# One 2 MB transfer for both up tiles of a group, and the down tiles' transfers issued from ScalarE's own queue

## The chip, the cores and the metric

One core of one Trainium2 chip. The time is device microseconds for one launch. Engines are named as in the profile: PE is TensorE's matmul side, PEld its weight loads, DVE is VectorE, ACT is ScalarE, POOL is GpSimd and SP is SyncE. "SPq" and "ACTq" are the parts of SyncE and ScalarE that issue DMA transfers.

## The reference

A first block (two layers of three kinds of attention) is followed by a second one of two layers with four token mixers each. The first of these has a dense feed-forward, the second a mixture of 8 experts in which each of 256 tokens goes to its best two. All data is 32-bit float. The change touches the mixture alone:

```python
logits = h @ router_w                       # 256 tokens, 8 experts
top_vals, top_idx = lax.top_k(logits, TOP_K)   # TOP_K = 2, softmax over the two
# every expert: (silu(h @ w1) * (h @ w3)) @ w2, D_MODEL = 1024, EXPERT_FF = 2816
```

The weights of the 8 experts are 8 x 3 x 1024 x 2816 x 4 bytes, 277 MB, and all of them are read once.

## The kernel before, in words

The mixture is the last stage. An expert's hidden width of 2816 is cut into 11 groups of 256 columns, so there are `UPS` = 88 groups. A group has three weight tiles of 128 partitions x 2048 floats (1 MB each, 8 KB of a row per partition): two *up* tiles (`w1` and `w3` for the first and the second half of the 1024 input features) and one *down* tile (`w2`). There are 264 tiles in all, numbered in the order in which PE uses them: `up_tile(g, 0)`, `up_tile(g, 1)`, then `down_tile(g - 2)`. So PE runs, in step g: the ups of group g, one transpose (`turn`) of the activations of group g-1, and the down of group g-2. ACT takes the tanh of a group when its ups are done, DVE multiplies the gates, ACT copies the transposed activations.

The experts are taken by rank of how many tokens they have (`TURN`). Of the eight turns, the third and the sixth are *heavy*: their expert has room for 128 tokens and not for 64, and its weights are cut in two parts, a rounded one made by ACT (L1020) and the rest made by DVE (L1200), for three matmuls in place of one. The other six turns are *light*. In time: two light turns (22 groups), one heavy (11), two light, one heavy, two light.

The tiles live in a ring of `RAW` = 12 places of 1 MB; four more places (`HI`) are used once, for the first 16 tiles. SyncE issues every transfer itself, in the order of the tiles, on its own queue (L981 to L994): tile n waits until PE has finished tile n-12 (n-16 for the first tiles behind the first 16). Each engine keeps its order of work; semaphore `m_done` counts the tiles that PE has finished. A transfer goes out as soon as its place is free:

```python
if n < FIRST:
    sp.wait_ge(family("m_done"), p * (TILES + FIRST) + n + 1)
else:
    sp.wait_ge(*tile_done(p, n - (FIRST if n < FIRST + RAW else RAW)))
src = ...
sp.dma_start(raw[slot_of(n)], src).then_inc(raw_loaded(p, n)[0], 16)
```

The first 12 places come free together in the last projection of the stage in front, at one increment of `m_done` by 12; the four of `HI` at another.

Of the kernel before, what the change touches and what calls it, by code (L numbers as in the profile page):

```python
# [17 lines left out]
P = 128  # L18
D = 1024
# [22 lines left out]
TURN = [0, 3, 1, 4, 5, 2, 6, 7]  # L42
PASSES = max(-(-min(SEQ, 2 * SEQ // max(r, 1)) // n) for r, n in enumerate(ROOMS))
W2B = 384
RAW = 12
HI = 4
FIRST = RAW + HI
HALF = NF // 2
# [84 lines left out]
def build(nc, a, consts, out, events):  # L133

    ccols, _, c_shared, c_first = constants()
    with ExitStack() as ctx:
# [179 lines left out]
        raw, raw_r = map(list, zip(*[carve_both(2048) for _ in range(6)]))  # L316
        top[0] = mark
        for i in range(5):
            raw.append(mem_ring[:, 2048 * i:2048 * (i + 1)])
            raw_r.append(carve_both(2048)[1])  # L320
# [3 lines left out]
        raw.append(mem_ring[:, top[0] - at_ring:top[0] - at_ring + 2048])  # L324
        raw_r.append(carve_both(2048)[1])
        assert top[0] <= after_z + c_all - c_first
        top[0] = 0
        assert len(raw_r) == RAW
        raw_hi, hi_r = map(list, zip(*[carve_both(2048) for _ in range(3)]))
        raw += raw_hi  # L330
# [3 lines left out]
        raw.append(sq.rearrange("p a b -> p (a b)")[:, 0:2048])  # L334
        assert len(hi_r) == HI
        he_f, he_h = high_places(KT, P)
        he = [carve(KT, GROUP) for _ in range(2)]
# [419 lines left out]

            return sum(heavy(k) for k in range(i))

        def slot_of(n):  # L760

            return n if n < FIRST else (n - FIRST) % RAW

        def raw_loaded(p, n):

            k = slot_of(n)
            if k >= RAW:
                last = max(range(k - RAW, len(chunks), NSLOT))
                s, before = at(f"w_loaded{k - RAW}", last)
                return s, p * 16 + before + 16  # L770
            loads = len(range(k, TILES - FIRST, RAW)) + 1
            return family(f"m_raw{k}"), p * 16 * loads + 16 * (1 if n < FIRST else (n - FIRST) // RAW + 2)

        def split_done(p, n):

# [10 lines left out]
        def moe_pe(pe, logit, open_group):  # L786
# [60 lines left out]
            def up(p, g):  # L847

                i, c = divmod(g, HALF)
                if g >= 2:  # L850
                    pe.wait_ge(family("m_hidden"), p * UPS + g - 1)
                for half in range(2):
                    n = up_tile(g, half)
                    if c == 0:
                        pe.wait_ge(family("m_he"), p * 2 * EXPERTS + 2 * i + (half + 1 if heavy(i) else 2))
                    if heavy(i):
                        pe.wait_ge(*split_done(p, n))
                        high, low = hi_r[SPLIT.index(n) % HI], raw_r[slot_of(n)]
                        for k in range(4):
                            kk = 4 * half + k  # L860
                            for j, (h_, w_) in enumerate(((he_h, high), (he_h, low), (he_l, high))):
                                ins = pe.matmul(ACC[g % 2][:, :], h_[:, kk, :], w_[:, 512 * k:512 * k + 512],  # L862
                                                start=(kk == 0 and j == 0), stop=(kk == KT - 1 and j == 2))
                    else:
                        pe.wait_ge(*raw_loaded(p, n))
                        for k in range(4):
                            kk = 4 * half + k
                            for f in range(2):
                                ins = pe.matmul(ACC[g % 2][64 * f:64 * f + 64, 0:2 * P], he[i % 2][:, kk, :],  # L869
                                                raw[slot_of(n)][:, 512 * k + 256 * f:512 * k + 256 * (f + 1)],  # L870
                                                start=(kk == 0), stop=(kk == KT - 1), skip_group_check=True)
                    ins.then_inc(family("m_done"), 1)

# [7 lines left out]
            def down(p, d):  # L881

                i, c = divmod(d, HALF)
                n = down_tile(d)
                pe.wait_ge(family("m_act"), p * UPS + d + 1)
                if c == 0 and i:
                    pe.wait_ge(family("m_y"), p * EXPERTS + i)
                if heavy(i):
                    pe.wait_ge(*split_done(p, n))
                    pe.wait_ge(family("m_act_low"), p * HEAVY * HALF + heavy_before(i) * HALF + c + 1)  # L890
                    high, low = hi_r[SPLIT.index(n) % HI], raw_r[slot_of(n)]
                    for f in range(2):
                        for half in range(2):
                            at_ = f * D + 512 * half
                            for j, (a_, w_) in enumerate(((act_h, high), (act_h, low), (act_l, high))):
                                ins = pe.matmul(SB[half][:, :], a_[:, d % 2, f * P:(f + 1) * P], w_[:, at_:at_ + 512],  # L896
                                                start=(c == 0 and f == 0 and j == 0),
                                                stop=(c == HALF - 1 and f == 1 and j == 2))
                else:
                    pe.wait_ge(*raw_loaded(p, n))  # L900
                    for f in range(2):
                        for half in range(2):
                            ins = pe.matmul(SB[0][64 * half:64 * half + 64, :], act_t[:, d % 2, GROUP * f:GROUP * (f + 1)],  # L903
                                            raw[slot_of(n)][:, f * D + 512 * half:f * D + 512 * half + 512],
                                            start=(c == 0 and f == 0), stop=(c == HALF - 1 and f == 1),
                                            skip_group_check=True)
                ins.then_inc(family("m_done"), 1)
# [69 lines left out]
        def moe_sync(sp):  # L977

            def body(p, learn):
                expert = {0: 0}  # L980
                for n in range(TILES):  # L981
                    g, j = TILE_ORDER[n]
                    i, c = divmod(g, HALF)
                    if i not in expert:
                        r = TURN[i]
                        if i == 1:
                            sp.wait_ge(*at("passes_known"))
                        expert[i] = sp.value_load(by_rank[0:1, r:r + 1], min_val=0, max_val=EXPERTS - 1)
                    if n < FIRST:
                        sp.wait_ge(family("m_done"), p * (TILES + FIRST) + n + 1)  # L990
# [4 lines left out]
                    if n == 2 * TILES // EXPERTS:  # L995
                        learn()
                        sp.dma_start(gain_row, a["final_norm_g_2"].rearrange("(r d) -> r d", r=1).broadcast_to((P, D)))\
                            .then_inc(family("m_gain_row"), 16)
            turns(sp, body)

        def moe_act(act):
# [13 lines left out]
            def high(p, n):  # L1015

                at_ = SPLIT.index(n)
                act.wait_ge(*raw_loaded(p, n))
                act.wait_ge(*tile_done(p, SPLIT[at_ - HI] if at_ >= HI else FIRST - 1))
                cp(hi_r[at_ % HI], raw[slot_of(n)]).then_inc(family("m_high"), 1)  # L1020

            def expert_in(p, i):

# [14 lines left out]
                ins.then_inc(family("m_y"), 1)  # L1038

            def body(p, learn):  # L1040
                for s in range(UPS + 2):
                    i, c = divmod(s, HALF)
                    if s == 2 * HALF:
# [6 lines left out]
                    if 1 <= s <= UPS:  # L1050
# [2 lines left out]
                        A(hid[g % 2][:, 0:n * P].rearrange("p (a b) -> p a b", a=n),  # L1053
                          ACC[g % 2][:, 0:2 * n * P].rearrange("p (a b) -> p a b", a=n)[:, :, 0:P], ACT.Tanh, scale=0.5)\
                            .then_inc(family("m_tanh"), 1)
                    if c == 2 and i:
                        y_out(p, i - 1)
                    if c == 9 and i + 1 < EXPERTS:
# [22 lines left out]
        def moe_dve(dve, st):  # L1081
# [114 lines left out]
            def low(p, n):  # L1196

                at_ = SPLIT.index(n)
                dve.wait_ge(family("m_high"), p * len(SPLIT) + at_ + 1)
                TTn(raw_r[slot_of(n)], raw[slot_of(n)], hi_f[at_ % HI], ALU.subtract).then_inc(family("m_split"), 1)  # L1200

            def expert_in(p, i):

# [1896 lines left out]
```

## Time and profile before

| | |
|---|---|
| median of 3 runs | 2174.63 us (2174.55 to 2176.81) |
| the profiled execution | 2175.69 us, span 2173.9 us |
| the mixture's weight stream | first issue at 1486.49, last tile's down matmuls begin at 2159.55 |
| PE busy in the span | 2070.3 us (95%) |
| DMA rate in the mixture | about 420 GB/s, against 225 GB/s over the span |

Times in the profile are microseconds from the start of the span. "DMA share" is the mean busy share of the core's 16 DMA engines and can be a little over 1, since packets overlap. For a DMA issue the profile gives the time from issue to landing, for which the transfers queued ahead of it on the same queue count too.

### The profile page before, as it was taken

Reading aid. Unit: us, or ns where it says so; the run is one execution under the profiler, and the core shown is the slowest. Engines: PE = TensorE matmul, PEld = TensorE weight load, DVE = VectorE, ACT = ScalarE, POOL = GpSimd, SP = SyncE. Lnnn points to the kernel's source line nnn. Section 1 sums busy time; section 2 is a strip of 40 time slices with the busy share of each in tenths; the row PEclk is TensorE's granted clock in tenths of the full one; section 3 lists DMA queues with packets and bytes.
Section 4 is the critical chain, followed back from the end, with each engine's and each line's share of the span. In section 5 each row is a group of like instructions: output and inputs, shape, how many; then the busy total and the mean of one; then the engine's idle time right before and its main releaser. Section 6 shows DMA issues by size and latency. Waiting matters only on the chain. (4 is left out here: it accounts for less than half of the span.)

```text
span 2173.9 us, 38831 instructions
## 1 busy us (share of the span) xinstructions
PE 2070.3 (95%) x15492; PEld 1737.7 (80%) x15492; DVE 1270.5 (58%) x2412; ACT 946.6 (44%) x1724; POOL 124.9 (6%) x115
## 2 busy tenths in 40 slices
PE   8999999999999999998999899998999999999997
PEld 7988888998978988888999888888556765568553
DVE  5465667565667776778665775777114931178211
ACT  5545544545554453446443544444014630065111
POOL 0100000010000024021000005012000000000000
PEclk9999999999999999999999999999999999999999
DMA  6443334444337444346554444339999999999997
GB/s 198 151 136 101 98 98 140 145 144 136 113 123 163 142 152 131 106 137 219 172 191 137 138 147 145 107 118 346 392 421 420 421 413 420 420 421 407 409 420 310
DMA packets 257818, 489.49 MB, mean 225 GB/s; under 512 B 35256, under 2 KB 208216, under 8 KB 223720
## 3 DMA queue, kind: packets, MB, share of 16 engines
q1 hardware_dynamic: 252112, 484.39, 61.6%
q8 instruction: 124, 2.03, 0.4%
q0 software_dynamic: 656, 1.80, 0.2%
q10 hardware_dynamic: 4872, 0.81, 0.2%
q14 instruction: 54, 0.44, 0.1%
HBM read 485.91 MB, written 1.05 MB: 224 GB/s over the span
## 5 line engine op out<-in xcount | busy, mean ns | idle before, releaser
L1356 PE MATMUL bank<-memr 128*128 128x256 f32 (+3 forms) x7056 | 896.6, 286 | 28.4 <-DVE memr L2417 9.7
L1356 PEld LDWEIGHTS bank<-memr 128*128 128x128 f32 (+2 forms) x7056 | 855.5, 185 | 58.8 <-issue 16.3
L2417 DVE TENSOR_TENSOR memr<-mem_low,memr 128x1024 fp32r<-128x1024 f32 (+3 forms) x328 | 400.0, 1238 | 63.8 <-ACT memr L1864 63.1
L1864 ACT CAST memr<-mem_low 128x1024 fp32r<-128x1024 f32 (+3 forms) x328 | 333.3, 1032 | 112.7 <-PE bank L1356 109.8
L1252 DVE SCALAR_TENSOR_TENSOR mem_high<-mem_high,bank 128x128 f32<-128x128 f32 (+1 forms) x88 | 28.0, 318 | 273.4 <-ACT mem_high L1053 273.4
L1053 ACT ACTIVATE mem_high<-bank 128x128 f32<-128x128 f32 (+1 forms) x88 | 26.7, 304 | 348.1 <-PE bank L869 322.8
L869 PE MATMUL bank<-mem_tail,mem_low 128*64 128x256 f32 x1088 | 127.5, 387 | 2.9 <-DMA mem_tail<-in_moe 2.3
L869 PEld LDWEIGHTS bank<-mem_tail,mem_low 128*64 128x64 f32 x1088 | 77.9, 139 | 54.2 <-issue 17.3
L660 PE MATMUL bank<-memr 128*128 128x256 f32 x960 | 115.6, 281 | 3.1 <-DVE memr L2436 3.1
L869 PE MATMUL bank<-mem_ring,mem_low 128*64 128x256 f32 x992 | 113.7, 381 | 3.7 <-DMA mem_ring<-in_moe 3.7
L660 PEld LDWEIGHTS bank<-memr 128*128 128x128 f32 x960 | 114.3, 189 | 3.5 <-issue 3.5
L869 PEld LDWEIGHTS bank<-mem_ring,mem_low 128*64 128x64 f32 x992 | 70.2, 137 | 49.3 <-issue 15.3
L862 PE MATMUL bank<-memr 128*128 128x512 f32 x272 | 91.2, 404 | 6.5 <-DVE memr_tail L1200 6.5
L2179 ACT ACTIVATE mem_high<-bank 128x256 f32<-128x256 f32 x64 | 24.4, 382 | 127.9 <-PE bank L1356 127.9
L2047 ACT ACTIVATE mem_high<-mem_high 128x144 f32<-128x144 f32 (+2 forms) x120 | 51.0, 425 | 58.9 <-DVE mem_high L2601 58.9
L1356 PE MATMUL bank<-memr_ring,memr 128*128 128x256 f32 (+2 forms) x540 | 71.0, 288 | 4.3 <-ACT mem_high L2026 3.6
L1200 DVE TENSOR_TENSOR memr_tail<-mem_tail,memr 128x2048 fp32r<-128x2048 f32 x26 | 59.3, 2287 | 26.9 <-ACT memr L1020 26.5
L1356 PEld LDWEIGHTS bank<-memr_ring,memr 128*128 128x128 f32 (+1 forms) x540 | 66.3, 181 | 8.9 <-issue 2.8
L862 PEld LDWEIGHTS bank<-memr 128*128 128x128 f32 x272 | 52.3, 192 | 22.3 <-DVE memr_tail L1200 7.6
L903 PE MATMUL bank<-mem_ring,mem_low 128*64 128x512 f32 x264 | 63.9, 605 | 1.5 <-DMA mem_ring<-in_moe 1.1
L629 PE MATMUL bank<-memr_ring 128*128 128x256 f32 x416 | 64.4, 282 | 0.0
L903 PE MATMUL bank<-mem_tail,mem_low 128*64 128x512 f32 x248 | 60.0, 604 | 1.1 <-ACT mem_low L1063 1.1
(367 smaller groups left out, 2815.6 us busy)
## 6 DMA issues: line engine op xcount, KB each, us to landing
mem_tail<-in_moe SPq DMA_DIRECT2D x132, 1024.0 KB, 15.4
mem_ring<-in_moe SPq DMA_DIRECT2D x128, 1024.0 KB, 16.2
mem_low<-in_w_in SPq DMA_DIRECT2D x112, 1024.0 KB, 5.2
mem_tail<-in_ffn_w SPq DMA_DIRECT2D x18, 1024.0 KB, 8.6
mem_low<-in_w_out SPq DMA_DIRECT2D x16, 1024.0 KB, 5.3
mem_low<-in_w_branch SPq DMA_DIRECT2D x12, 1024.0 KB, 5.0
mem_high<-in_ffn_w SPq DMA_DIRECT2D x12, 1024.0 KB, 8.1
mem_low<-in_w_branch SPq DMA_DIRECT2D x16, 512.0 KB, 3.5
```

Of the source, the lines that this page charges most:

```text
L629: ins = pe.matmul(YB[j // 2][:, (j % 2) * T:(j % 2 + 1) * T], w_[:, j * P:(j + 1) * P], a_, start=(F == 0 and j % 2 == 0 and i == 0), stop ...
L660: ins = pe.matmul(UB[F % 2][m][:, 0:T], w_[:, k, :], h_[:, k, 0:T], start=(k == 0 and i == 0), stop=(k == KT - 1 and i == (2 if F else 1)))
L862: ins = pe.matmul(ACC[g % 2][:, :], h_[:, kk, :], w_[:, 512 * k:512 * k + 512], start=(kk == 0 and j == 0), stop=(kk == KT - 1 and j == 2))
L869: ins = pe.matmul(ACC[g % 2][64 * f:64 * f + 64, 0:2 * P], he[i % 2][:, kk, :], raw[slot_of(n)][:, 512 * k + 256 * f:512 * k + 256 * (f + 1)],
L903: ins = pe.matmul(SB[0][64 * half:64 * half + 64, :], act_t[:, d % 2, GROUP * f:GROUP * (f + 1)], raw[slot_of(n)][:, f * D + 512 * half:f ...
L1053: A(hid[g % 2][:, 0:n * P].rearrange("p (a b) -> p a b", a=n), ACC[g % 2][:, 0:2 * n * P].rearrange("p (a b) -> p a b", a=n)[:, :, 0:P], A ...
L1200: TTn(raw_r[slot_of(n)], raw[slot_of(n)], hi_f[at_ % HI], ALU.subtract).then_inc(family("m_split"), 1)
L1252: S3(out=hid[2 + g % 2][:, 0:n * P].rearrange("p (a b) -> p a b", a=n), in0=hid[g % 2][:, 0:n * P].rearrange("p (a b) -> p a b", a=n), sca ...
L1356: ins = pe.matmul(out(bank), lhsT, rhs, start=((k, i) == order[0] and not half), stop=((k, i) == order[-1]), skip_group_check=half is not ...
L1864: cp(high, raw).then_inc(*sig("w_high", i))
L2047: st(A(sm[g % 2][0:nt, c:c + n], sm[g % 2][0:nt, c:c + n], ACT.Exp, scale=sc, bias=s_[0:nt, 3 + t:4 + t], accum_out=s_[0:nt, 6 + t:7 + t]) ...
L2417: st(V.tensor_tensor(low, raw, high, ALU.subtract), sig("w_split", i))
```

## The change

The two up tiles of a group lie side by side in memory on both sides, so that one transfer brings both: 2 MB, with rows of 16 KB per partition. The ring becomes four places for pairs and four for down tiles (`PAIRS` = 4, the same 12 MB); the four extra places hold pairs 4 and 5, once. SyncE issues the pairs, and the first four down tiles. Pair g waits until PE has finished *both* up tiles of the pair that held its place before, that of group g-4 (g-6 for groups 6 to 9), and both up tiles wait for the whole pair. Down tile g of group 4 and on is issued by ScalarE on its own queue in step g, behind the tanh of group g-1. It waits for nothing further, since by then PE has finished down tile g-4. In a heavy step ScalarE has two casts (L1020) of that step's up tiles ahead of the tanh.

```diff
-RAW = 12
+PAIRS = 4
+RAW = 3 * PAIRS
+LOAD_ORDER = [n for n in range(TILES) if TILE_ORDER[n][1] == 0 or TILE_ORDER[n][1] == 2 and TILE_ORDER[n][0] < PAIRS]
+LOAD_ORDER.sort(key=lambda n: (FIRST if PAIRS <= TILE_ORDER[n][0] < PAIRS + HI // 2 and TILE_ORDER[n][1] == 0 else n, n))
...
+        def pair_of(g):
+            return g if g < PAIRS + HI // 2 else (g - PAIRS - HI // 2) % PAIRS
...
         def raw_loaded(p, n):
-            k = slot_of(n)
...
+            g, j = TILE_ORDER[n]
+            if j == 2:
+                return family(f"m_down{g % PAIRS}"), 16 * (p * UPS // PAIRS + g // PAIRS + 1)
+            k = pair_of(g)
...
+            of_place = [q for q in range(UPS) if pair_of(q) == k]
+            return family(f"m_up{k}"), 16 * (p * len(of_place) + of_place.index(g) + 1)
+
+        def expert_of(eng, i):
+            r = TURN[i]
+            if i == 1:
+                eng.wait_ge(*at("passes_known"))
+            return eng.value_load(by_rank[0:1, r:r + 1], min_val=0, max_val=EXPERTS - 1)
...
-                for n in range(TILES):
+                for n in LOAD_ORDER:
...
+                    k = pair_of(g)
+                    if j < 2 and g >= PAIRS + HI // 2:
+                        sp.wait_ge(*tile_done(p, up_tile(max(q for q in range(g) if pair_of(q) == k), 1)))
                     else:
-                        sp.wait_ge(*tile_done(p, n - (FIRST if n < FIRST + RAW else RAW)))
-                    src = a["moe"][bass.DynSlice(expert[i], 1), c, j].rearrange("o p f -> (o p) f") if i else a["moe"][0, c, j]
-                    sp.dma_start(raw[slot_of(n)], src).then_inc(raw_loaded(p, n)[0], 16)
+                        sp.wait_ge(family("m_done"), p * (TILES + FIRST) + (FIRST if j < 2 and k >= PAIRS else RAW))
+                    if j == 2:
+                        sp.dma_start(single[g], weights(expert, i, c, 2)).then_inc(raw_loaded(p, n)[0], 16)
+                    elif k > PAIRS:
+                        for half in range(2):
+                            sp.dma_start(last_raw[half], weights(expert, i, c, 0)[:, 2048 * half:2048 * (half + 1)])\
+                                .then_inc(raw_loaded(p, n)[0], 16)
+                    else:
+                        sp.dma_start(wide_hi[:, 0:4096] if k == PAIRS else pair[k], weights(expert, i, c, 0))\
+                            .then_inc(raw_loaded(p, n)[0], 16)
...
                 for s in range(UPS + 2):
...
                             .then_inc(family("m_tanh"), 1)
+                    if PAIRS <= s < UPS:
+                        if i not in expert:
+                            expert[i] = expert_of(act, i)
+                        act.dma_start(single[s % PAIRS], weights(expert, i, c, 2)).then_inc(raw_loaded(p, down_tile(s))[0], 16)
```

## Rows read from the trace of the kernel before

**Rows 1.** Page, busy time of the engines over the span; DMA rate in 40 slices.

```profile
PE 2070.3 (95%) x15492; PEld 1737.7 (80%) x15492; DVE 1270.5 (58%) x2412; ACT 946.6 (44%) x1724; POOL 124.9 (6%) x115
GB/s 198 151 136 101 98 98 140 145 144 136 113 123 163 142 152 131 106 137 219 172 191 137 138 147 145 107 118 346 392 421 420 421 413 420 420 421 407 409 420 310
```

**Rows 2.** Windows: first heavy turn, second heavy turn, the stream's last stretch.

```profile
1669.00:1768.00 99.00, 98.58 (x476) 77.70 (x476) 82.14 (x75) 63.02 (x57) 0.00 (x0) 1.00 1.01 419
1910.00:2019.00 109.00, 108.39 (x508) 84.33 (x509) 87.43 (x79) 67.69 (x62) 0.00 (x0) 0.97 1.01 411
2132.00:2160.00 28.00, 23.08 (x145) 10.49 (x146) 2.50 (x8) 3.74 (x11) 0.00 (x0) 1.00 0.91 377
```

**Rows 3.** Chain that ended last: start, duration, work (or transfer waited for).

```profile
1639.41 25.35 DMA mem_tail<-in_moe
...
1878.80 27.16 DMA mem_tail<-in_moe
```

**Rows 4.** DMA view of 1800 to 1860, the queue's packets, MB and share.

```profile
q1 hardware_dynamic: 3455, 25.17, 100.9%
```

**Rows 5.** DMA view of 649.4 to 653.8, and window 650.5 to 652.5.

```profile
q0 software_dynamic: 127, 1.56, 83.5%
...
650.50:652.50 2.00, 1.59 (x14) 1.39 (x12) 1.90 (x3) 1.06 (x1) 0.00 (x0) 1.00 1.01 433
```

**Rows 6.** Timeline of SP, single issues: start, duration of issuing.

```profile
1486.49 0.34 SPq L994 DMA_DIRECT2D mem_tail<-in_moe  x1
...
1530.73 0.33 SPq L994 DMA_DIRECT2D mem_tail<-in_moe  x1
...
1561.05 0.33 SPq L994 DMA_DIRECT2D mem_tail<-in_moe  x1
...
1566.76 0.34 SPq L994 DMA_DIRECT2D mem_tail<-in_moe  x1
...
1736.88 0.33 SPq L994 DMA_DIRECT2D mem_tail<-in_moe  x1
...
1749.04 0.33 SPq L994 DMA_DIRECT2D mem_tail<-in_moe  x1
...
1757.59 0.33 SPq L994 DMA_DIRECT2D mem_ring<-in_moe  x1
...
1979.52 0.33 SPq L994 DMA_DIRECT2D mem_tail<-in_moe  x1
...
1988.13 0.33 SPq L994 DMA_DIRECT2D mem_tail<-in_moe  x1
...
2000.24 0.33 SPq L994 DMA_DIRECT2D mem_ring<-in_moe  x1
...
2008.87 0.33 SPq L994 DMA_DIRECT2D mem_ring<-in_moe  x1
...
2023.39 0.33 SPq L994 DMA_DIRECT2D mem_tail<-in_moe  x1
...
2132.68 1.93 SPq L994 DMA_DIRECT2D mem_ring<-in_moe  x1
```

**Rows 7.** Issue to landing, of those at 1486.49, 1566.76, 1736.88, 1979.52 and 2023.39.

```profile
mem_tail<-in_moe SPq DMA_DIRECT2D x1, 1024.0 KB, 4.8
...
mem_tail<-in_moe SPq DMA_DIRECT2D x1, 1024.0 KB, 9.5
...
mem_tail<-in_moe SPq DMA_DIRECT2D x1, 1024.0 KB, 13.5
...
mem_tail<-in_moe SPq DMA_DIRECT2D x1, 1024.0 KB, 11.3
...
mem_tail<-in_moe SPq DMA_DIRECT2D x1, 1024.0 KB, 7.9
```

**Rows 8.** Timeline of PE at the stream's end: last up tile, last two downs.

```profile
2152.05 1.95 PE L869 MATMUL bank<-mem_tail,mem_low 128*64 128x256 f32 x16 [0.45 <-DMA mem_tail<-in_moe]
...
2159.55 1.94 PE L903 MATMUL bank<-mem_ring,mem_low 128*64 128x512 f32 x8 [0.51 <-DMA mem_ring<-in_moe]
```

More of the change, by code:

```diff
@@ L315, in build @@
         top[0] = upper
-        raw, raw_r = map(list, zip(*[carve_both(2048) for _ in range(6)]))
+        pair, pair_r = map(list, zip(*[carve_both(4096) for _ in range(3)]))
         top[0] = mark
-        for i in range(5):
-            raw.append(mem_ring[:, 2048 * i:2048 * (i + 1)])
-            raw_r.append(carve_both(2048)[1])
+        pair.append(mem_ring[:, 0:4096])
+        pair_r.append(carve_both(4096)[1])
+        single, single_r = [], []
+        for i in range(2, 5):
+            single.append(mem_ring[:, 2048 * i:2048 * (i + 1)])
+            single_r.append(carve_both(2048)[1])
         htok = [carve(D)]
@@ L323, in build @@
         top[0] = -(-(after_z + ccols["decay"][0] - c_first) // 8) * 8
-        raw.append(mem_ring[:, top[0] - at_ring:top[0] - at_ring + 2048])
-        raw_r.append(carve_both(2048)[1])
+        single.append(mem_ring[:, top[0] - at_ring:top[0] - at_ring + 2048])
+        single_r.append(carve_both(2048)[1])
         assert top[0] <= after_z + c_all - c_first
         top[0] = 0
-        assert len(raw_r) == RAW
-        raw_hi, hi_r = map(list, zip(*[carve_both(2048) for _ in range(3)]))
-        raw += raw_hi
+        assert len(pair_r) == len(single_r) == PAIRS
+        wide_hi, wide_hi_r = carve_both(6144)
+        hi_r = [wide_hi_r[:, 2048 * i:2048 * (i + 1)] for i in range(3)]
         hi_f = [v.bitcast(F32) for v in hi_r]
@@ L333, in build @@
         hi_r.append(memr_squares[:, 0:2048])
[L334 removed]
+        last_raw = wide_hi[:, 4096:6144], sq.rearrange("p a b -> p (a b)")[:, 0:2048]
         assert len(hi_r) == HI
@@ L758, in heavy_before, with raw_tile, raw_tile_r, weights @@
             return sum(heavy(k) for k in range(i))
-        def slot_of(n):
-            return n if n < FIRST else (n - FIRST) % RAW
-        def raw_loaded(p, n):
-            k = slot_of(n)
[L767 to L772, printed above, removed]
+        def pair_of(g):
+            return g if g < PAIRS + HI // 2 else (g - PAIRS - HI // 2) % PAIRS
+        def raw_tile(n, singles=single, pairs=pair, rest=(wide_hi[:, 0:4096], last_raw)):
+            g, j = TILE_ORDER[n]
+            if j == 2:
+                return singles[g % PAIRS]
+            k = pair_of(g)
+            if k > PAIRS:
+                return rest[1][j]
+            return (rest[0] if k == PAIRS else pairs[k])[:, 2048 * j:2048 * (j + 1)]
+        def raw_tile_r(n):
+            return raw_tile(n, single_r, pair_r)
+        def raw_loaded(p, n):
+            g, j = TILE_ORDER[n]
+            if j == 2:
+                return family(f"m_down{g % PAIRS}"), 16 * (p * UPS // PAIRS + g // PAIRS + 1)
+            k = pair_of(g)
+            if k >= PAIRS:
+                last = max(range(k - PAIRS, len(chunks), NSLOT))
+                s, before = at(f"w_loaded{k - PAIRS}", last)
+                return s, before + 16 * (k - PAIRS + 1) * (p + 1)
+            of_place = [q for q in range(UPS) if pair_of(q) == k]
+            return family(f"m_up{k}"), 16 * (p * len(of_place) + of_place.index(g) + 1)
+        def weights(expert, i, c, j):
+            lo, f = (0, 4096) if j < 2 else (P * 4096, 2048)
+            if i == 0:
+                return a["moe"][0, c, lo:lo + P * f].rearrange("(p f) -> p f", f=f)
+            return a["moe"][bass.DynSlice(expert[i], 1), c, lo:lo + P * f].rearrange("o (p f) -> (o p) f", f=f)
+        def expert_of(eng, i):
[3 more added lines that the diff above has]
+            return eng.value_load(by_rank[0:1, r:r + 1], min_val=0, max_val=EXPERTS - 1)
         def split_done(p, n):
@@ L1040, in body @@
             def body(p, learn):
+                expert = {0: 0}
                 for s in range(UPS + 2):
@@ L3080 @@
     w1, w3, w2 = (arrays.pop(f"moe_w{i}_2")[0] for i in (1, 3, 2))
[L3081 removed]
+    moe = np.empty((EXPERTS, HALF, 3 * P * 2048), np.float32)
+    ups, downs = moe[..., 0:P * 4096].reshape(EXPERTS, HALF, P, 2, 4, 2, 2, P), moe[..., P * 4096:]
     for m, w in enumerate((w1, w3)):
[L3083 to L3085 removed]
+        ups[..., m, :] = w.reshape(EXPERTS, 2, 4, P, HALF, 2, P).transpose(0, 4, 3, 1, 2, 5, 6)
+    downs[:] = w2.reshape(EXPERTS, HALF, 2, P, D).transpose(0, 1, 3, 2, 4).reshape(EXPERTS, HALF, P * 2 * D)
     arrays["moe"] = moe
```

28 lines of the change are left out of this document (11 added, 17 removed).

## The prediction

> **What bounds the kernel now.** First the page. PE is busy 95% of the span, which would make it the bound, but the slices of DMA rate say something else for the last third: from the 29th slice on the rate stands at 407 to 421 GB/s, against 98 to 219 before [rows 1]. The mixture reads 277 MB, and 264 tiles of 1.049 MB at 421 GB/s are 657 us of the 673 us between the first issue and the last down. So this stage is a stream of weights.
>
> Next the chain of waits. It stands on a DMA for 25 us at the end of the first two light turns and for 27 us at the end of the next two [rows 3]; behind the last two light turns PE is idle in 28 - 23.1 = 5 us [rows 2]. The chain's 25 us are the whole life of one transfer, with ten others queued ahead of it, and not an idle stretch. A light group asks 5.6 us of PE and 3 x 2.49 = 7.5 us of the stream; a heavy one 8.6 us of PE (issues of the same kind of tile lie that far apart, 1979.52 to 1988.13 [rows 6]). So in light turns PE catches up with the stream until it starves, and in heavy turns the stream gets ahead until it runs out of free places. How near it comes to that is told by issue to landing. A transfer that finds the queue empty lands in 4.8 us, 2.3 us more than its own 2.49 [rows 7]; late in the heavy turns it takes 13.5 us (1736.88) and 11.3 us (1979.52), and just behind the second one 7.9 us at 2023.39 [rows 7]. There is little queued there, and the second heavy window shows it as 411 GB/s against 419 in the first [rows 2].
>
> The end is therefore: start of the stream, plus bytes over rate, plus every stretch in which the stream has no transfer, plus what follows the last landing.
>
> **The change part by part.** Against the profiled execution, 2175.69 us.
>
> *Longer packets.* A row of 8 KB is one packet: 25.17 MB are 3072 of them, and 100.9% of 16 x 60 us over 3072 is 315 ns each [rows 4]; the small packets that count the semaphores bring that to 314. The trace has one transfer with longer rows, 13,952 bytes: 112 of its packets are the 1.56 MB of q0, in 83.5% of 16 x 4.4 us, so 525 ns each [rows 5]. A line through both gives 614 ns for 16,384 bytes, 8 x 614 against 16 x 314 per DMA engine: 0.11 us less per pair. Bounds: nothing, and 2.097 MB at the 433 GB/s of rows 5 in place of 421, 0.14 us. I take 0.11. But the gain only counts where the stream isn't afterwards held by free places.
>
> *Fewer, larger and later issues.* Before, places come free one by one, 1 MB each. Now the three transfers of a step leave together, when PE has finished a group's second up tile: the pair from SP, and the down tile from ACT right behind the tanh. At that moment as much has been issued as before. But until the next such moment, 5.6 us (light) or 8.6 us (heavy) later, nothing is added, where two more tiles went out before. If the queue holds less than that interval plus the 2.3 us of a fresh start, the stream runs dry. I go through the three places.
>
> Start. PE ends its first group at 1530.73 and the first pair goes out then, where next to nothing of the 16 early tiles is left in the queue. Its bytes flow from 1533.0. Four pairs and the downs 4 to 6 (11 MB, 26.9 us) are through at 1559.9, with the first of the rest not issued until 1561.05, when group 6 has ended (a place of the ring is needed again) [rows 6]: dry until 1563.3. Two groups (6 MB, 14.7 us) are then landed at 1578.1. Before, that tile, issued at 1566.76, landed at 1576.2 [rows 6, 7]: 2.0 us later. I take +3.0, as this tally lets each fresh start run at full rate at once (bounds 1 and 5). Thirteen pairs follow until PE starves: -1.4, so the stream is 1.6 late.
>
> First heavy turn. It begins starved, and the first cast now waits for a whole pair, 2.5 us more, and its down tile comes late too; I take 3.0 more (bounds 2 and 5). PE is 4.6 late in it, the stream, after twelve more short pairs, 0.3. The tile issued at 1736.88 landed at 1750.4, so now 1750.7. The next end of an up pair is 1749.04 (PE gathers the next expert's tokens in between, so the interval is 12.2 us), now 1753.6, and bytes flow from 1755.9: dry for 5.2 us. Three tiles take 7.35; the next, 1757.59, is 1764.5 against 1763.3: dry for 1.2 [rows 6, 7]. The stream is now 6.7 late. Before lost nothing here.
>
> Second heavy turn. Nineteen pairs give back 2.1: the stream is 4.6 late, PE 7.6, and by 1980 the stream 3.8. The tile of 1979.52 (landed 1990.8) lands at 1994.6; the next moment, 1988.13, gives bytes from 1998.0, dry 3.4, and they end at 2005.4; 2000.24 gives 2010.1, dry 4.7, end 2017.5; 2008.87 gives 2018.8, dry 1.3. Two more groups end at 2040.8 where the tile of 2023.39 landed at 2031.3 [rows 6, 7]. The stream is 9.5 late. Before had dry moments of some 3 us of its own in this place, which is why the difference is less than the sum.
>
> Last light turns. Sixteen pairs give back 1.8: last landing 7.7 late.
>
> Tail. Before, the last tile landed at 2159.4, and after it came one down, 1.94 us, since all else was done: the last up tile had begun at 2152.05 [rows 8]. From its end at 2153.9 on, PE's order holds three downs, two transposes and an expert's turn, 7.0 us without waits. With two queues it matters who is served. If both take turns by packets, a pair (8 packets per engine) and a down (8 shorter ones) end together, so the downs, which are issued with the pair of three groups ahead, reach PE late: pair 87 lands with down 84, and downs 85 to 87 follow in 7.5 us. PE then does down 84 (1.9), up 87 (3.5) and the 7.0: 12.4 - 7.5 = 4.9 us behind the last landing, against 2.1 before. That is +2.8. Bounds: 0, if ACT's transfers always come last, and 3.5 + 7.0 - 2.1 = 8.4, if the last pair is the last to land. No row has both queues full, so I take the case between.
>
> The Trainium skill, "DMA: Bandwidth & Descriptors", section "Queues, rings and completion order", has it that each DMA engine goes round the queue rows that have work, a packet at a time. No stretch before shows two full queues; by this rule the tail is +2.8, by order of issue it would be nearer to the upper bound.
>
> *ACT's issues.* 84 of them at about 0.34 us as SP's [rows 6], 29 us in all, beside an ACT that is busy in 63 of 99 us of a heavy turn [rows 2]: hidden in PE's 8.6 us a group, and in a light turn more so. If an issue holds ACT as long as the 1.93 us of SP's at a full queue [rows 6], it isn't; see below. SP's saved issues cost nothing before and save nothing.
>
> Sum: 7.7 + 2.8 = +10.5 us. The profiled execution is 1.1 us over the median; counted from it the sum gives 2186.2, and from the median, which I take, 2174.6 + 10.5, about **2185 us**.
>
> **The rivals.**
> A, *the queue never runs dry.* Then all 88 pairs save 0.11, 9.7 us, less 2.8 of tail: 2167.7, faster. It decides at the last up pair ahead of a gather: the queue must hold 12.2 + 2.3 = 14.5 us there. The rows say 13.5 and less. Only if pairs saved far more, or if PE were later, is it otherwise. 8%. The Trainium skill, same page, section "Measured (HBM→SBUF, 128 partitions, SWDGE, issued from GpSimd)", speaks for it: its rates rise with the size of a transfer, 341 GB/s at 1 MB and 425 at 16 MB. The trace has 421 at 1 MB, back to back, so most of that rise isn't there to be had.
> B, *the losses are there but half as large, and cancel.* Dry time of 3.0 + 6.4 + 9.4 less before's own 3 is 15.8; half of it, 7.9, against the 67 pairs counted above at 0.14, 9.4, and 2.8 of tail: +1.3, or 2176, and between 2173 and 2178. For it speaks that the delays at a heavy turn's start are estimates; against it the intervals between the ends of up pairs, which are read off rows. 9%.
> C, *ACT is held.* At 1.93 us per issue a heavy step of ACT is 63/11 + 1.6 = 7.3 us, in one chain with DVE's 82/11 = 7.5; with the casts late by 1.6 the heavy groups could grow by 0.5 to 1: another 8 to 20 us, 2193 to 2205. For it speaks the 1.93, against it that it comes only with some ten transfers queued and ACT's queue holds three or four. 9%.
> D, the forecast: 74%, its own range 2179 to 2192.
>
> **How the numbers follow.** About 0.2% (4 us) is what a measurement here can tell from no change. A and a part of B are faster: 10%; the rest of B within: 7%; C, D: 83% slower. The range leaves out A, a piece of B, and most of C: 2176 to 2196.
>
> **What would show it.** Windows of 10 us with a DMA share clearly below 1 at 1530 to 1565, about 1750 to 1765 and about 1995 to 2020 (the dry moments); elsewhere 424 to 427 GB/s. The page should show about 11,000 packets fewer at the same MB. The first heavy turn's matmuls begin 4 to 5 us later, the last up pair's matmuls end some 2 us ahead of the last landing. The last landing is at about 2167. I am wrong if the share stays at 1.01 through the heavy turns' ends (A), if ACT issues take over 1 us (C), or if the rate itself moves by more than 2% either way with two queues.

## The result and the profile after

The median went from 2175.72 us (2174.55 to 2179.02) to 2194.55 us (2192.39 to 2197.70), a ratio of 1.0089 with a 95% interval of 1.0076 to 1.0102: 16.5 to 22.2 us slower. The forecast was 2185, with a range of 2176 to 2196. The time lies in the range, and the direction is right; the size is off by 9.5 us.

The page of the kernel after, its busy times, rates and packets, answers to [rows 1]:
```profile
PE 2073.1 (95%) x15492; PEld 1746.1 (80%) x15492; DVE 1270.6 (58%) x2412; ACT 948.4 (43%) x1724; POOL 124.9 (6%) x115
GB/s 201 145 137 97 97 97 147 155 132 140 116 128 158 137 160 110 115 168 179 173 183 162 139 154 116 97 168 336 398 425 425 391 371 425 425 425 356 415 425 299
DMA packets 245287, 489.45 MB, mean 223 GB/s; under 512 B 33864, under 2 KB 206824, under 8 KB 222328
```
Every engine is as busy as before (the page does not count the issuing of DMAs as busy). Undisturbed slices move 425 GB/s where they had 420 or 421. But slices at the ends of the heavy turns have 391, 371 and 356, where [rows 1] has 407 at the least. The windows show it more sharply (the first three answer to [rows 2], the others are 10 us each; the last two columns are the DMA share and GB/s):
```profile
1669.00:1768.00 99.00, 97.31 (x445) 76.10 (x444) 81.19 (x69) 61.66 (x52) 0.00 (x0) 0.98 0.94 385
1910.00:2019.00 109.00, 106.73 (x535) 80.65 (x534) 85.47 (x74) 67.74 (x61) 0.00 (x0) 1.00 0.96 394
2132.00:2160.00 28.00, 23.82 (x172) 13.47 (x172) 4.15 (x13) 2.11 (x8) 0.00 (x0) 1.00 1.01 426
1530.00:1540.00 10.00, 10.00 (x79) 6.19 (x77) 1.38 (x5) 0.79 (x3) 0.00 (x0) 0.88 0.59 215
1750.00:1760.00 10.00, 10.00 (x63) 8.76 (x62) 6.14 (x5) 6.71 (x7) 0.00 (x0) 1.00 0.62 263
2010.00:2020.00 10.00, 10.00 (x46) 8.09 (x45) 9.60 (x8) 5.47 (x5) 0.00 (x0) 1.00 0.60 220
```
The stream runs dry in the three places that the prediction named. PE's waits in the whole mixture (source line, what it waited for: us in total, times, longest) show something that it didn't name:
```profile
PE bank L940 <- DMA mem_ring<-in_moe: 27.0, 19, 2.1
PE bank L899 <- DVE memr_tail L1248: 4.5, 3, 1.7
PE bank L933 <- DVE memr_ring L1248: 1.5, 3, 0.8
PE bank L906 <- DVE mem_low L1259: 0.6, 1, 0.6
```
L940 is the down. In the light turns PE starves for down tiles and never for up tiles; at the heavy turns it also waits for DVE's part of them (L899, L933). Its timeline in the second light turn shows one round of it: the down waits 1.82 us, and the ups in front of it ran without a wait, since their pair lay there already.
```profile
1641.74 1.94 PE L940 MATMUL bank<-mem_ring,mem_low 128*64 128x512 f32 x8 [1.64 <-DMA mem_ring<-in_moe]
1643.51 3.62 PE L906 MATMUL bank<-mem_tail,mem_low 128*64 128x256 f32 x32
1647.06 0.33 PE L915 MATMUL bank<-mem_high 128*128 128x128 f32 x1
1649.21 1.94 PE L940 MATMUL bank<-mem_ring,mem_low 128*64 128x512 f32 x8 [1.82 <-DMA mem_ring<-in_moe]
```
Such a pair lies in its place unused until the down has come.

Three issues of pairs, at the start and at a dry moment, with their rows of the DMA view (size, us from issue to landing); they answer to [rows 6, 7]:
```profile
1533.20 0.33 SPq L1035 DMA_DIRECT2D mem_tail<-in_moe  x1
...
1563.52 0.33 SPq L1035 DMA_DIRECT2D mem_tail<-in_moe  x1
...
1759.36 0.33 SPq L1035 DMA_DIRECT2D mem_tail<-in_moe  x1
```
```profile
mem_tail<-in_moe SPq DMA_DIRECT2D x1, 2048.0 KB, 8.9
...
mem_tail<-in_moe SPq DMA_DIRECT2D x1, 2048.0 KB, 11.6
mem_ring<-in_moe ACTq DMA_DIRECT2D x1, 1024.0 KB, 11.8
...
mem_tail<-in_moe SPq DMA_DIRECT2D x1, 2048.0 KB, 11.5
mem_ring<-in_moe ACTq DMA_DIRECT2D x1, 1024.0 KB, 11.7
```
The first of them goes out 2.47 us later than its counterpart at 1530.73 [rows 6]. That isn't the change's doing: over the executions profiled here the first group of the mixture ended between 3.1 us earlier and 2.5 us later than in before's. I take 2.5 us out wherever this execution is compared with before's, so of its 19.0 us (2194.67 less 2175.69) 16.5 are left to explain. A whole kernel that does what before does (control_halves, below) still comes out 1.4 to 2.0 us late in such a comparison, so figures from single executions are good to about 2 us.

### The profile page after: what moved, and what is told of

Its sections match the earlier page's. It is cut to its first block, busy times and chain, and to the rows that moved or that the text cites. A ratio compares the mean times of both kernels' runs of the same rounds, so it can differ in the third digit from the quotient of the medians.

```text
span 2192.9 us, 38439 instructions
## 1 busy us (share of the span) xinstructions
PE 2073.1 (95%) x15492; PEld 1746.1 (80%) x15492; DVE 1270.6 (58%) x2412; ACT 948.4 (43%) x1724; POOL 124.9 (6%) x115
## 4 chain that ended last, share of the span: by engine, by line
PE 36%; DMA 9%; DVE 5%; ACT 2%; issue 1%; POOL 1%; ACTq 0%; DVEq 0%; POOLq 0%; SPq 0%
PE bank L1404 7%; DMA mem_ring<-in_moe 7%; PE bank L906 7%; PE bank L666 5%; PE bank L899 5%; PE bank L940 3%; PE bank L635 3%; PE bank L933 3%; DMA mem_tail<-in_moe 2%; DVE memr L2465 1%; PE bank L860 1%; POOL mem_high L1837 1%; PE bank L915 1%; PE bank L546 0%; ACT memr L1912 0%
## 5 line engine op out<-in xcount | busy, mean ns | idle before, releaser
L906 PE MATMUL bank<-mem_tail,mem_low 128*64 128x256 f32 x1536 | 178.0, 385 | 0.6 <-DVE mem_low L1259 0.6
L906 PEld LDWEIGHTS bank<-mem_tail,mem_low 128*64 128x64 f32 x1536 | 112.7, 139 | 68.3 <-issue 22.7
L940 PE MATMUL bank<-mem_ring,mem_low 128*64 128x512 f32 x528 | 128.5, 607 | 27.0 <-DMA mem_ring<-in_moe 27.0
L899 PE MATMUL bank<-memr 128*128 128x512 f32 x272 | 90.7, 402 | 4.5 <-DVE memr_tail L1248 4.5
L940 PEld LDWEIGHTS bank<-mem_ring,mem_low 128*64 128x64 f32 x528 | 33.3, 136 | 73.9 <-issue 59.6
L899 PEld LDWEIGHTS bank<-memr 128*128 128x128 f32 x272 | 51.8, 191 | 20.2 <-DVE memr_tail L1248 6.4
L1062 ACT CAST memr<-mem_tail 128x2048 fp32r<-128x2048 f32 x26 | 49.2, 1906 | 28.8 <-DMA mem_tail<-in_moe 17.2
L1248 DVE TENSOR_TENSOR memr_ring<-mem_ring,memr 128x2048 fp32r<-128x2048 f32 x24 | 54.7, 2288 | 10.6 <-ACT memr L1062 10.6
```

Source lines behind the costliest of these rows:

```text
L1062: cp(hi_r[at_ % HI], raw_tile(n)).then_inc(family("m_high"), 1)
L1248: TTn(raw_tile_r(n), raw_tile(n), hi_f[at_ % HI], ALU.subtract).then_inc(family("m_split"), 1)
```

## The experiments

Apart from act_early, the kernels share one rewrite of SyncE's loop: it goes through a list of transfers sorted by the step of PE that frees their place. A kernel differs by what stands in the list.
```diff
+def free_at(g):
+    return g - PAIRS if g >= 2 * PAIRS + HI // 2 else g - PAIRS - HI // 2
...
+for g in range(PAIRS + HI // 2, UPS):
+    if g in APART:
+        PLAN += [(free_at(g) - 0.5, 0, g), (free_at(g), 1, g)]
+    else:
+        PLAN.append((free_at(g), 3, g))
+if DOWN_SP:
+    PLAN += [(d - 1 + 0.1 if DOWN_LATE else d - 2 + 0.2, 2, d) for d in range(PAIRS, UPS)]
```
A group in APART gets its two up tiles as before, 1 MB each, each issued when its own half of the place is free and waited for alone. DOWN_SP puts the down tiles on SyncE's queue, DOWN_LATE at ScalarE's moment (when the group in front has its ups done), otherwise when down tile g-4 is done, about a group earlier. PARTS = 2 issues a pair as two transfers of 1 MB at one moment. The first six pairs are never taken apart. The results:

| kernel | ups | downs | median us | ratio (95%) |
|---|---|---|---|---|
| after | pairs | ACT, late | 2194.55 | 1.0089 (1.0076 to 1.0102) |
| one_queue | pairs | SP, late | 2191.63 | 1.0076 (1.0055 to 1.0097) |
| act_early | pairs | ACT, early | 2187.29 | 1.0048 (1.0033 to 1.0062) |
| one_queue_early | pairs | SP, early | 2182.62 | 1.0036 (1.0022 to 1.0049) |
| halves_apart | apart | ACT, late | 2191.82 | 1.0073 (1.0054 to 1.0093) |
| two_halves | 2 x 1 MB at once | ACT, late | 2207.97 | 1.0150 (1.0127 to 1.0173) |
| one_queue_halves | 2 x 1 MB at once | SP, late | 2198.52 | 1.0100 (1.0085 to 1.0115) |
| control_halves | apart | SP, early | 2176.75 | 1.0005 (0.9996 to 1.0014) |
| apart_at_dry | mixed | SP, early | 2181.81 | 1.0024 (1.0012 to 1.0036) |
| apart_at_heavy | mixed | SP, early | 2178.09 | 1.0011 (1.0002 to 1.0021) |
| deep_pairs | mixed | SP, early | 2173.47 | 0.9989 (0.9980 to 0.9998) |

Before was measured beside them: 2174.35 us with one_queue, one_queue_early, two_halves and halves_apart, 2175.18 with act_early, one_queue_halves, control_halves and deep_pairs, 2175.91 with the last two, 2175.72 with after. Where two kernels stand in different sets, the ratios compare better than the medians, and the two can differ by some 2 us. A second table has how late PE is in the profiled executions: the start of the tanh of groups 30, 60 and 87 (end of the first heavy turn, within the second, last group) against before's, less each execution's own offset at group 0, in us. The execution of act_early is the slowest of its four (2190.47), that of deep_pairs the fastest of its eleven (2169.28), so the row of the first is likely too high at its end and that of the second too low.

| kernel | 30 | 60 | 87 |
|---|---|---|---|
| after | 7.9 | 11.6 | 17.8 |
| one_queue | 7.8 | 12.8 | 19.7 |
| act_early | 6.9 | 10.9 | 14.9 |
| one_queue_early | 4.5 | 6.4 | 8.1 |
| halves_apart | 6.3 | 11.5 | 18.7 |
| two_halves | 11.4 | 23.0 | 33.6 |
| one_queue_halves | 8.8 | 16.0 | 24.0 |
| control_halves | 1.9 | 1.4 | 2.0 |
| apart_at_dry | 3.3 | 4.6 | 5.8 |
| apart_at_heavy | 0.9 | 0.7 | 3.0 |
| deep_pairs | 0.7 | -2.5 | -3.5 |

**one_queue** (`DOWN_SP = True, DOWN_LATE = True`).

> As the changed kernel, but SyncE issues the down tiles too, each right behind the pair of three groups ahead and with ScalarE's moment (both up tiles of the group in front done). Only the second queue is gone. Theory 1 (what costs is the moment of issue: three tiles leave together and the queue runs dry before the next): the dry stretches stay, only the lag of the down tiles at a heavy turn's start (about 2 us) and the tail (2.4 us) go; about 2190 us, 4 to 5 less than the changed kernel's 2194.5. Theory 2 (two full queues that share the DMA engines cost the time): most of the 19 us goes, 2180 or less. Theory 3 (ScalarE is held by issuing): same as theory 2.

It is 2.9 us under the kernel after, with overlapping intervals, and as late by the second table: most of the loss is there without the second queue. Theories 2 and 3 (2180 or less) are out; theory 1 had 2190. How the late down tiles bring it in is seen at the first of them that ScalarE has to cut. Down 22 is issued at 1658.79 and lands 22.6 us later; ACT idles 3.12 us for it, with the tanh of group 24 queued behind the casts, and PE 2.38 us for DVE's part. In before the cast of the same tile (1677.82) had no wait. ACT's and PE's timelines of one_queue:
```profile
1681.49 1.90 ACT L1097 CAST memr<-mem_ring 128x2048 fp32r<-128x2048 f32 x1 [3.12 <-DMA mem_ring<-in_moe]
```
```profile
1685.85 0.49 PE L955 MATMUL bank<-memr 128*128 128x512 f32 x1 [2.38 <-DVE memr_ring L1277]
```
Against before's, less the offset, the tanh of group 23 is 1.9 us late and that of group 24, on which the next issues hang, 5.9.

**one_queue_early** (the same with `DOWN_LATE = False`).

> As one_queue, but a down tile is issued as soon as its own place is free (the down tile four groups before is done), one group earlier than ScalarE did. Pairs as in the changed kernel. Theory 1: the queue holds up to 1 MB (2.5 us) more at the ends of both heavy turns and at the start; another 4 to 6 us less than one_queue, about 2185. Theory 2: no different from one_queue by more than 2 us.

The moment of the down tiles alone is worth 9.0 us, more than theory 1 gave it (4 to 6). What stays, +8.3, is the price of the pairs, less what their long rows win. PE waits for no down tile here, but for whole pairs (L928), 12.4 us in 9 waits, 10.7 in 8 of them as below, and at the heavy turns for DVE's part of them:
```profile
PE bank L928 <- DMA mem_tail<-in_moe: 10.7, 8, 1.7
PE bank L921 <- DVE memr_tail L1277: 9.6, 2, 4.8
```

**two_halves** (the kernel after with `PARTS = 2`: 8 KB rows, ACT's queue kept).

> As the changed kernel, but every pair from group 6 on goes out as two transfers of 1 MB with rows of 8 KB, back to back at the same moment, and PE still waits for both. Only the long rows are gone. If the long rows save 0.11 us a pair where the stream is not dry (some 50 pairs): 4 to 6 us slower than the changed kernel, 2199. If long rows make a fresh start slow (a lone pair took 8.9 us from issue to landing, 1.7 more than 2.3 + 4.9): up to 1.7 us back at each of some eight fresh starts, 2188 to 2194.

This is the largest miss: 13.4 us over the kernel after, where 4 to 6 were expected. The DMA view of 1600 to 1650, two_halves first, then the kernel after (count, KB, median us to landing):
```profile
mem_tail<-in_moe SPq DMA_DIRECT2D x12, 1024.0 KB, 23.2
mem_ring<-in_moe ACTq DMA_DIRECT2D x8, 1024.0 KB, 9.5
```
```profile
mem_tail<-in_moe SPq DMA_DIRECT2D x6, 2048.0 KB, 22.0
mem_ring<-in_moe ACTq DMA_DIRECT2D x8, 1024.0 KB, 21.6
```
With 16 KB rows on one queue and 8 KB rows on the other, downs and ups take as long. With 8 KB on both, the downs are through in 9.5 us and the ups, twice as many, wait behind them. PE then starves for ups (34.3 us in 27 waits), where it starved for downs.

**halves_apart** (`APART` all groups from 6, downs left to ACT: the down tiles' part of the change alone).

> As the changed kernel, but from group 6 on each up tile goes out by itself, as soon as its half of the place is free, with a semaphore of its own, so that PE waits for a half. Down tiles stay with ScalarE. Theory 1: half of the missing transfers are back in the queue at each end of a heavy turn and at the start, and a heavy turn starts on a half again: 10 to 14 us less than the changed kernel, less the 5 us that the long rows gave: 2182 to 2188. Theory 2 (queues): it stays above 2190.

Theory 1 fell; it stayed above 2190, as theory 2 had it. The down tiles' part alone costs 17.5 us, the pairs' part alone 8.3 (each median against before's beside it), both together 18.8. They don't add up. But this kernel does not lose its time where the kernel after does. Its DMA view of 1600 to 1650 and PE's largest wait in the mixture (L928 is the ups) are those of two_halves:
```profile
mem_tail<-in_moe SPq DMA_DIRECT2D x10, 1024.0 KB, 26.3
mem_ring<-in_moe ACTq DMA_DIRECT2D x7, 1024.0 KB, 9.3
```
```profile
PE bank L928 <- DMA mem_tail<-in_moe: 21.4, 21, 2.3
```
With 8 KB rows on both queues the downs overtake the ups, and PE starves for ups: it is 7.3 us late at group 21, still in the light turns, where one_queue_early is 2.8.

**act_early** (the kernel after, ScalarE issuing before it casts; the same issue behind the tanh is gone):
```diff
+                    if PAIRS <= s < UPS:
+                        ...
+                        act.wait_ge(*tile_done(p, down_tile(s - PAIRS)))
+                        act.dma_start(single[s % PAIRS], weights(expert, i, c, 2)).then_inc(raw_loaded(p, down_tile(s))[0], 16)
                     if s == 0:
                         expert_in(p, 0)
```

> The kernel after, with ScalarE still issuing the down tiles on its own queue, but at the start of step s, as soon as PE has finished down tile s-4, about one group earlier than behind the tanh. Theory (the moment of the down tile's issue costs half of the loss, the second queue nothing): as one_queue_early, 2183 us, 2179 to 2187, that is 9 to 13 us under the kernel after; three matched windows (1720 to 1790 and 1980 to 2050) at a DMA share of 0.95 or more. Rival 1 (the two queues sharing by packets delays the pairs, whenever the downs are issued): 2190 or more. Rival 2 (a wait in ScalarE's program ahead of the casts delays the heavy turns): above the kernel after, 2197 or more, with ACT's idle ahead of the casts larger by over 0.5 us a group.

The gain is 7.3 us by the medians and 8.9 by the ratios, at or just under the least that the theory called for (9); rival 1's 2190 is not met. The windows 1720 to 1790 and 1980 to 2050 have a DMA share of 0.93 each, not 0.95. It is 4.7 us over one_queue_early by the medians, 2.6 by the ratios, with overlapping intervals, so that the times alone do not show that two queues cost anything here. The traces show a place where they do, the start of the first heavy turn. ACT's first casts of two consecutive pairs, groups 22 and 23, in before, after and one_queue_early:
```profile
1656.12 1.90 ACT L1020 CAST memr<-mem_tail 128x2048 fp32r<-128x2048 f32 x1 [5.36 <-DMA mem_tail<-in_moe]
...
1664.79 1.91 ACT L1020 CAST memr<-mem_tail 128x2048 fp32r<-128x2048 f32 x1 [3.75 <-DMA mem_tail<-in_moe]
```
```profile
1664.07 1.90 ACT L1062 CAST memr<-mem_tail 128x2048 fp32r<-128x2048 f32 x1 [4.63 <-DMA mem_tail<-in_moe]
...
1675.12 1.90 ACT L1062 CAST memr<-mem_tail 128x2048 fp32r<-128x2048 f32 x1 [6.75 <-DMA mem_tail<-in_moe]
```
```profile
1659.42 3.70 ACT L1097 CAST memr<-mem_tail 128x2048 fp32r<-128x2048 f32 x2 [8.37 <-DMA mem_tail<-in_moe]
...
1668.01 1.91 ACT L1097 CAST memr<-mem_tail 128x2048 fp32r<-128x2048 f32 x1 [4.29 <-DMA mem_tail<-in_moe]
```
On one queue the two are 8.6 us apart, as in before 8.7. With two queues it is 11.1, here and in act_early (1661.77 and 1672.88): in the kernel after, a down tile issued at 1658.70 lands at 1675.00 and pair 23, issued at 1647.32, 0.1 us behind it: the down has had turns that pair 23 needed. What let it in lies between pairs 22 and 23 on SyncE's queue, as it does in before: the gain of the last normalization, 512 KB in 128 rows of 4 KB. In the kernel after it is issued at 1641.43 and lands 26.3 us later, 3.8 behind pair 22 and 7.4 ahead of pair 23. The queues' rows (packets, MB, share) while its rows pass, 1663 to 1667:
```profile
q10 hardware_dynamic: 129, 0.92, 55.0%
q1 hardware_dynamic: 140, 0.84, 51.2%
```
**one_queue_halves** (one_queue with `PARTS = 2`).

> As one_queue (SyncE issues the down tiles too, at the late moment, one queue in order), but each pair goes out as two transfers of 1 MB with rows of 8 KB at the same moment. It parts the length of the rows from the sharing between queues: two_halves had both changed, at +13 us. Theory (the +13 was the down queue taking half of the bytes while the ups starve): the short rows alone cost what my term of 0.11 us per pair gives where the stream is the bound, 88 x 0.11 = 9.7 at most and 3 to 5 where it is not held by free places, so 2194 to 2198 against one_queue's 2191.6, and downs and ups land in the order of their issues. Rival (short rows cost by themselves, on any queue): 2203 to 2208.

It took 2198.5, 0.5 above the theory's upper edge. Short rows cost 6.9 us on one queue by the medians (5.2 by the ratios, whose intervals overlap), and the second queue 9.5 more with 8 KB rows (two_halves), clear of noise, against 2.9 with 16 KB, which is not.

**control_halves** (`DOWN_SP = True`, all apart: before's scheme in the new layout).

> The new layout of the places and SyncE's one queue, but every up tile behind the first six groups is issued by itself when its own half is free and every down tile when its own place is free: the scheme of before in the new code. Theory: 2174 to 2177, no difference from before. If it is above 2178, something of the layout or of the program itself (the order of the first 18 transfers, the waits for halves) is part of the loss, and the terms found with one_queue_early must be lowered by it.

There is no difference from before that shows (0.05%). The layout costs nothing.

**apart_at_dry and apart_at_heavy** (one_queue_early with `APART` at 6 to 11, 33 to 42, 66 to 76, and at 21 to 25, 54 to 58).

> one_queue_early with single up tiles, each issued at its own half's moment, only at the start and at the ends of the heavy turns (groups 6 to 11, 33 to 42, 66 to 76); pairs of 2 MB elsewhere, the starts of the heavy turns too. Theory (most of one_queue_early's 8.3 us is dry time at the ends of the heavy turns): 2175 to 2178, that is 5 to 6 us of the 8.3 gone. Rival (the loss is made at the starts of the heavy turns, where PE waits for whole pairs): 2179 to 2182.

> one_queue_early with single up tiles only around the starts of the heavy turns (groups 21 to 25 and 54 to 58). Theory: 2 to 4 us of the 8.3 gone, 2179 to 2181, with the dry windows at the heavy turns' ends still there. Rival (the loss is made at the starts of the heavy turns): 2174 to 2177, and the first heavy turn's matmuls begin where the kernel before has them.

My theory fell. apart_at_dry came at the rival's number; apart_at_heavy lies below the theory's range and 1.1 above the rival's, with PE where the rival had it. By the ratios, the single tiles at the dry moments take 2.6 of one_queue_early's 7.8 us away (36 to 24 ten-thousandths, with overlapping intervals), those at the heavy turns' starts 5.4 (36 to 11, intervals just apart). By the second table PE is 0.9 late in the first heavy turn in place of 4.5, and with it goes most of the rest: the DMA share of 1750 to 1760, 0.63 in one_queue_early, is 0.92, though the pairs at that place are whole in both.

**deep_pairs** (`APART` at both and at 86, 87; 43 of the 82 groups stay pairs, not the 42 that the numbers below imply).

> One queue by SyncE, down tiles issued when their own place is free, and pairs of 2 MB only where the queue is deep; groups 6 to 11, 21 to 25, 33 to 42, 54 to 58, 66 to 76, 86 and 87 go out as single up tiles when each half is free (40 of 82 groups). Theory: the loss of one_queue_early (8.3 us) comes all from those places, and the 48 pairs save 0.11 us each where the stream is the bound: 2174.4 less 1 to 4, so 2170 to 2174. Rival (pairs cost in light turns too, since PE waits for a whole pair where it starves): 2177 to 2181.

It is the fastest kernel here, within the theory's range: 0.9989 (0.9980 to 0.9998), faster than before by 2.4 us with an interval that ends just under 1, and within the 0.2% that counts as no change. Against control_halves in the same runs it is 3.3 us faster.

## Why the prediction was right in kind and short in size

Its own steps, each against the profiled execution, less the 2.5 us:

| step | predicted | measured |
|---|---|---|
| stream at the start | +3.0 | +3.8 |
| stream at the end of the second light turn | +1.6 | +3.0 |
| PE in the first heavy turn | +4.6 | +7.9 |
| stream behind the first dry stretch | +6.7 | +11.5 |
| stream ahead of the second heavy turn | +4.6 | +10.2 |
| PE in the second heavy turn | +7.6 | +11.5 |
| stream behind the second dry stretch | +9.5 | +15.9 |
| last landing | +7.7 | +14.1 |
| tail | +2.8 | +2.4 |
| sum | +10.5 | +16.5 |

**Longer packets: right.** The pairs of groups 11 to 21 win back 0.105 us each (the landing of a group's last up tile goes from 6.29 to 5.24 us behind before's), those of the fourth light turn 0.106; the term was 0.11. In an undisturbed stretch the queues' rows (packets, MB, share of 16 engines' time) are, for 1800 to 1860, against [rows 4]:
```profile
q1 hardware_dynamic: 1166, 16.96, 66.5%
q10 hardware_dynamic: 1166, 8.46, 33.9%
```
16.96 MB are 1035 packets of 16 KB, and 66.5% of 16 x 60 us over them is 617 ns; the line through [rows 4, 5] gave 614.

**Turns by packets: right.** Pair and down land together (11.5 and 11.7 us). That the two rows above have 1166 packets each doesn't show it, since a group asks for 128 rows of either kind. What shows it are stretches in which more is asked of one queue: the 129 and 140 packets at the heavy turn's start above, and two_halves, where SyncE's queue has two rows of 8 KB to move for each of ScalarE's, from 1604 to 1608:
```profile
q10 hardware_dynamic: 110, 0.89, 53.3%
q1 hardware_dynamic: 112, 0.79, 47.3%
```
This is what the Trainium skill, "DMA: Bandwidth & Descriptors", section "Queues, rings and completion order", says of an engine that goes round the queues that have work. The trace agrees, with one row of 4, 8 or 16 KB as a packet. The tail followed: pair 87 landed at 2168.61, the downs 85 to 87 up to 2176.03, in 7.4 us against 7.5, and the tail came to 2.4. But I applied the rule to the tail alone. At a heavy turn's start it lets a down tile issued 11.4 us after pair 23 land with it, for 2.4 us.

**The delay at a heavy turn's start: a step that failed.** "I take 3.0 more (bounds 2 and 5)" came out as 4.9 in the first heavy turn: PE 7.9 late, the stream 3.0. 2.5 of it are the wait for a whole pair, which I had (first cast 7.9 us behind before's, stream 5.5, both with the offset in), and 2.4 the down that overtook pair 23 (second cast 10.3 behind). I had turns by packets and never asked what short rows on SyncE's queue would do. "Its down tile comes late too" had no term of its own. It hardly shows here because pair 23 is later still, but without the second queue it takes that place: one_queue is 7.8 late by ACT's wait for down 22. Issued a group earlier, the downs spare 9.0 us on one queue and some 7 to 9 on two. one_queue_early is 4.5 late where the sum to there is 4.6; this is in part luck, since its stream is 0.9 late there and not 1.6. PE's lateness sets the moments of all issues of the turn's eleven groups, and where the stream is dry it passes into it one for one. At the second heavy turn the delay was 1.3 (PE 11.5, stream 10.2), less than the 3.0 taken.

**What a dry stretch adds: the other step that failed.** Beyond PE's lateness the two dry stretches were to add 2.1 and 1.9 us to the stream's (6.7 less 4.6, 9.5 less 7.6). They added 3.6 and 4.4. The 6.4 us by which the stream was short behind the second one (15.9 against 9.5) are therefore: 1.4 from the start and the pairs behind it, 1.9 from the first heavy turn's delay, 1.5 from the first dry stretch, 0.8 from pairs that gave back 1.3 between the stretches and not 2.1, less 1.7 at the second heavy turn's start, and 2.5 from the second dry stretch. The tail takes 0.4 off. So 4.0 of the 6.0 missing us are the price of the dry stretches, and the two delays nearly cancel as errors of the forecast (1.9 and -1.7), though what is lost at the heavy turns' starts is the larger part of the loss itself (5.4 of 7.8 us with early downs, apart_at_heavy).

The likely reason is that a fresh start was priced too low. 3 MB in two transfers issued together on an empty queue were to need 2.3 + 7.35 = 9.65 us. The kernel after shows 11.7 (1759.36) and 10.6 (2014.31), one_queue 10.0 from the pair's issue. There the pair itself is 2.9 us earlier than at 2014.31 of the kernel after (7.5 against 10.4), since it doesn't share. Its rows for 1997.86 (pair) and 1998.37 (down):
```profile
mem_tail<-in_moe SPq DMA_DIRECT2D x1, 2048.0 KB, 7.5
...
mem_ring<-in_moe SPq DMA_DIRECT2D x1, 1024.0 KB, 9.5
```
At 0.9 us or more each, two or three in a dry stretch would make the 1.5 and 2.5 us. That is argued from these durations; no run takes it apart.

**ACT's issues: right.** They take 0.36 us in the mean and 0.38 at most, and moving all 84 to SyncE changes 2.9 us, within noise. Rival C is out. Rival A is out by the shares of 0.60 and 0.62. Rival B is out as a forecast (2173 to 2178), but what it said of the dry moments was not far off: where the starts of the heavy turns are repaired and the pairs kept at the dry moments (apart_at_heavy), losses and gains leave +2.4 us.

**Open.** What the second queue costs in the whole change: 2.9 us between after and one_queue, and 4.7 or 2.6 between act_early and one_queue_early, each with overlapping intervals, though 2.4 us of it are seen in the casts. And why the two parts cost 17.5 and 8.3 alone and 18.8 together. One part of an answer is that PE's lateness at the heavy turns is common to both and is paid once. Another is that halves_apart, with 8 KB rows on both queues, pays for the downs' larger share, which the long rows take away again when both parts are there: the second queue costs 9.5 us beside pairs in 8 KB rows and 2.9 beside 16 KB. No run parts the two. Missing is a kernel with single up tiles and late downs on SyncE's queue, which would price the late moment alone.

## What to carry to other kernels

When transfers are made larger or moved to another engine, ask of each tile how far ahead of its use it is issued, not only whether the queue stays full: here issuing the down tiles a group later cost 9.0 us on one queue, and keeping the merged transfers at the dry moments 2.6. Where a second queue shares the engines, look for transfers with short rows on the first: each of their rows gives the other queue a turn. Merge transfers where the queue is deep, and leave them single where a consumer starves or places come free one by one. Where a slower phase begins behind a starved one, a wait at that point is carried through to the end.

## What the runs showed of the hardware that was not expected

- A queue's share of the bytes goes with its packets' size. With 16 KB rows on SyncE's queue and 8 KB on ScalarE's, ups and downs took 22.0 and 21.6 us from issue to landing; with 8 KB on both 23.2 and 9.5, and the kernel lost 13.4 us with the same bytes and queues (5 to 7 of them the short rows cost on one queue too).
- A 512 KB transfer in rows of 4 KB on one queue let a whole 1 MB down tile of the other queue pass, 129 packets beside 140, and delayed the pair behind it by 2.4 us.
- A pair issued on an empty queue with nothing behind it needs 8.9 us at 1533.20, and 7.5 us at 1997.86 of one_queue with a down issued right behind it. What makes the difference was not tried.
- The two parts of the change, alone, cost 17.5 and 8.3 us, and together 18.8.
